# A hybrid encoder step on one core: normed tokens split in place, layer 1's weight sums started later, turned probabilities copied earlier

## The reference

```python
h = rmsnorm(x, g_pre_mix)
z = h @ w_in                       # B, C, xin | c_q, c_kv, k_rope | gate_conv, gate_mla
y_a = B * causal_conv3(C * xin)
y_b = latent_attention(...)        # 8 heads, chunk-causal mask, rotary key, cache for the sample
x = x + rmsnorm((sigmoid(ga) * y_a + sigmoid(gb) * y_b) @ w_o, g_post_mix)
x = x + rmsnorm(square(relu(rmsnorm(x, g_pre_ffn) @ w1)) @ w2, g_post_ffn)
```

## Time and profile before

| | |
|---|---|
| median of three runs (lowest, highest) | 1723.73 us (1723.25, 1723.80) |
| time of the profiled execution | 1726.3 us |
| its span, first to last instruction | 1724.5 us |
| PE busy | 1705.7 us (99%) |
| DVE busy | 1309.3 us (76%) |
| ACT busy | 855.1 us (50%) |
| POOL busy | 122.3 us (7%) |
| mean granted TensorE clock | 0.997 of full speed |

### The profile page before, as it was taken

One profiled execution on the slowest core, in us unless ns is written; L12 is line 12 of the kernel. 1 busy time (PEld: TensorE's weight loads), 2 busy tenths in 40 slices (PEclk: granted clock), 3 DMA queues, 4 the chain that ended last, 5 costly groups with the idle time before them and its releaser, 6 DMA issues.

```text
span 1724.5 us, 31894 instructions
## 1 busy us (share of the span) xinstructions
PE 1705.7 (99%) x12735; PEld 1690.9 (98%) x12735; DVE 1309.3 (76%) x2514; ACT 855.1 (50%) x1665; POOL 122.3 (7%) x163
## 2 busy tenths in 40 slices
PE   9999999999999999999999999999999999999997
PEld 9998999999999999999999999999999999999997
DVE  7788787767798786668687797777678887777665
ACT  7625454545465454436366364545435536444452
POOL 1412121212210000000001000000000000000000
PEclk9999999999999999999999999999999999999998
DMA  7899898898762232323124454343532213322231
GB/s 239 198 212 244 214 209 211 178 249 235 163 129 97 89 96 86 99 86 111 60 84 149 148 166 139 114 121 112 171 117 98 99 37 111 98 86 87 74 99 55
DMA packets 90996, 231.54 MB, mean 134 GB/s; under 512 B 9824, under 2 KB 25440, under 8 KB 90848
## 3 DMA queue, kind: packets, MB, share of 16 engines
q1 hardware_dynamic: 71968, 185.45, 33.5%
q0 software_dynamic: 17600, 41.95, 13.8%
q10 hardware_dynamic: 1280, 2.10, 0.3%
HBM read 214.39 MB, written 57.02 MB: 157 GB/s over the span
## 4 chain that ended last, share of the span: by engine, by line
PE 94%; DMA 2%; DVE 2%; ACT 1%; SPq 1%; issue 0%; DVEq 0%; ACTq 0%
PE ring L811 19%; PE ring L813 19%; PE ring L812 19%; PE att L811 11%; PE att L813 11%; PE att L812 11%; PE att L3527 1%; DMA cache_pe_raw<-cache_pe_in 1%; PE att L806 1%; PE att L805 1%; DMA small_raw<-small_in 1%; DMA xs_lo_raw<-h_kept 1%; PE att L818 0%; ACT rope_s L1291 0%; PE att L3343 0%
## 5 line engine op out<-in xcount | busy, mean ns | idle before, releaser
L811 PE MATMUL ring<-xs_hi,w_lo 128*128 128x288 f32 x1872 | 556.6, 297 | 4.3 <-DVE xs_lo L2744 2.2
L813 PE MATMUL ring<-xs_hi,w_hi 128*128 128x288 f32 x1872 | 551.4, 295 | 0.0
L812 PE MATMUL ring<-xs_lo,w_hi 128*128 128x288 f32 x1872 | 551.3, 294 | 0.0
L2071 DVE TENSOR_TENSOR w_lo<-w_raw,w_hi 128x1024 fp32r<-128x1024 f32 (+1 forms) x364 | 370.0, 1035 | 37.3 <-ACT w_hi L1220 27.2
L811 PEld LDWEIGHTS ring<-xs_hi,w_lo 128*128 128x128 f32 x1872 | 351.6, 188 | 7.3 <-DVE ga L2355 2.4
L812 PEld LDWEIGHTS ring<-xs_lo,w_hi 128*128 128x128 f32 x1872 | 351.7, 188 | 1.4
L813 PEld LDWEIGHTS ring<-xs_hi,w_hi 128*128 128x128 f32 x1872 | 351.5, 188 | 0.0
L813 PE MATMUL att<-f_hi,w_hi 128*128 128x288 f32 x960 | 283.2, 295 | 0.0
L812 PE MATMUL att<-f_lo,w_hi 128*128 128x288 f32 x960 | 282.9, 295 | 0.0
L811 PE MATMUL att<-f_hi,w_lo 128*128 128x288 f32 x960 | 282.6, 294 | 0.0
L811 PEld LDWEIGHTS att<-f_hi,w_lo 128*128 128x128 f32 x960 | 180.4, 188 | 0.0
(11 more groups left out here) (342 smaller groups left out, 3184.4 us busy)
## 6 DMA issues: line engine op xcount, KB each, us to landing
w_raw<-blocks_in SPq DMA_DIRECT2D x195, 512.0 KB, 3.7
weight_sums<-blocks_in POOLq DMA_DIRECT2D x80, 256.0 KB, 7.2
w_raw<-blocks_in SPq DMA_DIRECT2D x62, 256.0 KB, 4.6
weight_sums<-blocks_in POOLq DMA_DIRECT2D x20, 512.0 KB, 5.6
weight_sums<-weight_sums POOLq DMA_DIRECT2D x40, 256.0 KB, 7.6
w_raw<-weight_sums SPq DMA_DIRECT2D x20, 512.0 KB, 4.6
w_raw<-weight_sums SPq DMA_DIRECT2D x40, 256.0 KB, 4.4
small_raw<-small_in SPq DMA_DIRECT2D x16, 320.0 KB, 4.6
```

The lines of the kernel that those rows point to most:

```text
L811: pe.matmul(out, w[1], x[0], start=first, stop=False)
L812: pe.matmul(out, w[0], x[1], start=False, stop=False)
L813: return pe.matmul(out, w[0], x[0], start=False, stop=last)
L2071: return dve.tensor_tensor(out, a, hi.bitcast(F32), ALU.subtract)
```

## The change

The normed tokens are no longer stored and loaded back: ACT and DVE split them from `x` where they lie, in the order (0, 0), (4, 0), (0, 1), (4, 1) of half tiles. For this, in mixed head 2, the first two products come ahead of the projections on PE; the turned tiles are copied in head 2, each when the part of `x` under it has been split; their four low parts are made by DVE in head 2 as well, as is the weight of position 2, which was split at the end of head 1. Three low parts of the normed tokens are made at the end of head 1. In all plain heads ACT copies the turned probabilities ahead of the next weight and the small weights. POOL makes layer 1's ten sums only when head 7 of layer 0 has had its merged rows back. In head 7 the natural cache (`naraw`) is split behind the merged rows for w_o, the copy for the convolution comes ahead of the cache's sample columns, and the low parts of seven merged rows come ahead of the eighth.

```diff
@@ H_ORDER
-H_ORDER = ((0, 0), (4, 0), (4, 1), (0, 1))
+H_ORDER = ((0, 0), (4, 0), (0, 1), (4, 1))
@@ SP
-            def h_load(n):
...
-            def h_store(n):
...
-                if h == 1:
-                    sp.wait_ge(pl.h_made, KC * (L + 1))
...
-                    if (h, j) == (FIRST_MIXED - 1, 4):
-                        sp.wait_ge(pl.ring_full, full(L, r_hd(h, 4, 0)))
-                        sp.wait_ge(pl.h_stored, 48 * (L + 1))
-                        h_load(0)
-                        h_load(1)
-                        sp.wait_ge(pl.ring_full, full(L, r_hd(h, 4, 1)))
-                        h_load(2)
-                        h_load(3)
-                    elif is_mixed(h):
+                    if is_mixed(h):
@@ POOL
-        sums_steps(0, BEFORE_KEYS)
+        sums_steps(0, BEFORE_KEYS, 0, 2 * MIXED)
...
             if L == 0:
-                sums_steps(BEFORE_KEYS, N_SUMS + 2)
+                sums_steps(BEFORE_KEYS, 2 * MIXED + 2, 0, 2 * MIXED)
+                pool.wait_ge(pl.sums_third, 16 * 2 * MIXED)
+                pool.wait_ge(pl.my_landed, 64)
+                sums_copy(2 * MIXED)
+                sums_steps(2 * MIXED, N_SUMS + 2, 2 * MIXED, N_SUMS)
@@ ACT, plain_head
                 exponents(h)
+                turned_hi(h)
                 next_weight(2)
                 small_hi(L, h + 1)
-                turned_hi(h)
...
+                eng.wait_ge(pl.ring_free, ring_freed(3, 1))
+                apart()
+                conv_begin(h)
+                if h == HEADS - 1:
                     eng.wait_ge(pl.latent_lo, L * 4 + 4)
...
-                    eng.wait_ge(pl.nat_landed, L * 16 + 16)
-                    act.activation(pl.nah[:, :, :], pl.naraw[:, :, :], ACT.Copy).then_inc(pl.cache_hi, 1)
-                eng.wait_ge(pl.ring_free, ring_freed(3, 1))
-                apart()
-                conv_begin(h)
-                next_weight(3)
-                if h == FIRST_MIXED - 1:
-                    eng.wait_ge(pl.turn_made, 4 * (L + 1))
-                    eng.wait_ge(pl.h_stored, 48 * (L + 1))
-                    for t in TURN_ORDER:
-                        act.activation(pl.th[t][:, :, :], pl.traw[t][:, :, :], ACT.Copy).then_inc(pl.turn_hi, 1)
-                else:
+                if h != FIRST_MIXED - 1:
+                    next_weight(3)
                     next_weight(4)
@@ ACT, mixed_head
                 def normed_hi(n):
...
-                    eng.wait_ge(pl.h_landed[n], 16 * (L + 1))
-                    act.activation(pl.xh[tile], pl.xlraw[tile], ACT.Copy).then_inc(pl.h_hi, 1)
+                    eng.wait_ge(pl.ring_full, full(L, r_hd(h - 1, 4, half)))
+                    eng.wait_ge(pl.h_made, KC * (L + 1))
+                    act.activation(pl.xh[tile], pl.x[tile], ACT.Copy).then_inc(pl.h_hi, 1)
+
+                def turned_hi_of(i):
+                    t = TURN_ORDER[i]
+                    eng.wait_ge(pl.turn_made, 4 * (L + 1))
+                    eng.wait_ge(pl.h_lo, 4 * L + (3 if t < 2 else 4))
+                    act.activation(pl.th[t][:, :, :], pl.traw[t][:, :, :], ACT.Copy).then_inc(pl.turn_hi, 1)
 
                 def even_projections():
                     for half in range(2):
                         rotary_swap(h, half)
                     if h == FIRST_MIXED:
-                        normed_hi(0)
+                        turned_hi_of(1)
                     keys_hi(h)
                     rotary_hi(h)
...
                     if h == FIRST_MIXED:
-                        normed_hi(2)
+                        turned_hi_of(2)
+                        turned_hi_of(3)
+                        pos_hi(L, at + 2)
...
                 if h == FIRST_MIXED:
+                    for n in range(4):
+                        normed_hi(n)
+                    turned_hi_of(0)
+                    snapshot(0)
                     even_projections()
                     pos_hi(L, at + 3)
-                    normed_hi(3)
-                    snapshot(0)
@@ ACT, after weight_hi(L, n_wo(4), ...)
+            eng.wait_ge(pl.nat_landed, L * 16 + 16)
+            act.activation(pl.nah[:, :, :], pl.naraw[:, :, :], ACT.Copy).then_inc(pl.cache_hi, 1)
@@ DVE, plain_head
-                next_weight(3)
+                if h != FIRST_MIXED - 1:
+                    next_weight(3)
                 if h < FIRST_MIXED - 1:
                     next_weight(4)
-                elif h == FIRST_MIXED - 1:
-                    head_mix_lo(0)
-                    head_mix_lo(1)
 
                 attention_out(h)
 
                 own.wait()
+                if h == FIRST_MIXED - 1:
+                    normed_head_lo(0)
                 if h < HEADS - 1:
                     gated_out(h, 0)
+                    if h == FIRST_MIXED - 1:
+                        normed_head_lo(1)
                     gated_out(h, 1)
+                    if h == FIRST_MIXED - 1:
+                        normed_head_lo(2)
@@ DVE, mixed_head
                     rotary_sum(h, 0)
                     rotary_sum(h, 1)
+                    keys_lo(h)
                     if h == FIRST_MIXED:
-                        normed_head_lo(0)
-                    keys_lo(h)
+                        head_mix_lo(0)
                     rotary_lo(h)
-                    if h == FIRST_MIXED:
-                        normed_head_lo(1)
                     values_lo(h, 0)
                     values_lo(h, 1)
                     if h == FIRST_MIXED:
-                        head_mix_lo(2)
+                        head_mix_lo(1)
...
                 if h == FIRST_MIXED:
+                    upper_left(0, pl.cv[:, cols(0)])
+                    normed_head_lo(3)
                     even_projections()
+                    pos_lo(L, at + 2)
+                    head_mix_lo(2)
                     head_mix_lo(3)
-                    upper_left(0, pl.cv[:, cols(0)])
+                    first_difference(0)
                     pos_lo(L, at + 3)
-                    first_difference(0)
-                    normed_head_lo(2)
                     second_sum(0)
-                    normed_head_lo(3)
@@ DVE, w_o
+            for k in range(HEADS - 1):
+                merged_lo(x_part(L, X_WOA + k), k, cols(0))
             k = HEADS - 1
             gated_out(k, 0)
...
-            for k in range(HEADS - 1):
-                merged_lo(x_part(L, X_WOA + k), k, cols(0))
...
             weight_lo(L, n_wo(4), SLOT_WO[4])
+            cache_lo(2, pl.nal[:, :, :], pl.naraw[:, :, :], pl.nah[:, :, :])
@@ PE, mixed_head
-                if h == FIRST_MIXED:
-                    projections(h)
-                for i in range(4):
+                ahead = 2 if h == FIRST_MIXED else 4
+                for i in range(ahead):
                     product(h, 0, i)
-                if h != FIRST_MIXED:
-                    projections(h)
-                for i in range(4, 7):
+                projections(h)
+                for i in range(ahead, 7):
                     product(h, 0, i)
```

More of the change, by code:

```diff
@@ L954, in pos_load @@
                     sp.dma_start(pl.half_slot(s, k)[2], piece).then_inc(pl.slots[s], 16)
-            def h_load(n):
-                k0, half = H_ORDER[n]
-                sp.dma_start(pl.xlraw[:, k0:k0 + 4, cols(half)], pl.h_kept[:, k0:k0 + 4, cols(half)]) \
-                    .then_inc(pl.h_landed[n], 16)
-            def h_store(n):
-                rows = slice(3 * n, min(3 * n + 3, KC))
-                sp.dma_start(pl.h_kept[:, rows, :], pl.x[:, rows, :]).then_inc(pl.h_stored, 16)
             def my_load(n):
@@ L1014, in _ @@
                             pos_load(q)
-                    if h == FIRST_MIXED - 1 and j < 3:
-                        h_store(j)
                     if h == HEADS - 1:
@@ L1142, in sums_add_third, with sums_steps @@
             pool.dma_start(pl.sums[n][:, 3, :], pl.sums[n][:, 0, :], accum_op=ALU.add).then_inc(pl.sums_third, 16)
-        def sums_steps(n0, n1):
+        def sums_steps(n0, n1, first, end):
             for n in range(n0, n1):
-                if n < N_SUMS:
+                if n < end:
                     pool.wait_ge(pl.sums_copied, 48 * (n + 1))
-                if 1 <= n <= N_SUMS:
+                if first < n <= end:
                     pool.wait_ge(pl.sums_first, 32 * n)
-                if 2 <= n <= N_SUMS + 1:
+                if first + 1 < n <= end + 1:
                     pool.wait_ge(pl.sums_second, 16 * (n - 1))
-                if n >= 3:
+                if n > first + 2:
                     pool.wait_ge(pl.sums_third, 16 * (n - 2))
-                if n + 1 < N_SUMS:
+                if n + 1 < end:
                     sums_copy(n + 1)
-                if n < N_SUMS:
+                if n < end:
                     sums_add_first(n)
-                if 1 <= n <= N_SUMS:
+                if first < n <= end:
                     sums_add_second(n - 1)
-                if n >= 2:
+                if n > first + 1:
                     sums_add_third(n - 2)
```

(16 more changed lines are left out.)

4 lines of the change are left out of this document (removed).

## The result

| | before | after |
|---|---|---|
| median of six runs each (lowest, highest) | 1723.76 us (1723.25, 1729.72) | 1732.65 us (1730.76, 1735.46) |
| time of the profiled execution, its span | 1726.3, 1724.5 us | 1732.8, 1731.0 us |
| PE busy | 1705.7 us | 1709.6 us |
| mean granted TensorE clock | 0.997 | 0.995 |

The ratio after to before is 1.0039 (95% interval 1.0026 to 1.0052), 6.7 us by the ratio. The changed kernel is slower. The prediction was 1726.4 us with a range up to 1729.5, and the time lies above it.

What follows compares the result with a forecast made beforehand. PE, busy 1705.7 of 1724.5 us, was taken as the bound, with only 6.8 us of standstills to win. Terms -2.4 + 1.2 + 2.9 - 2.2 + 3.2 = +2.7 us on the median 1723.7 gave 1726.4 us, range 1719.5 to 1729.5.

Steps and rivals of the forecast that it cites:

- Turned probabilities, -2.4: Layer 0, head 1: copied ahead of the small weights, their low parts end before PE asks; 2.4 us of wait go.
- Head 2, layer 0, +1.2: Scores at T + 27.1 instead of T + 25.9, T being the end of head 1's last block's first half; 1.2 us lost.
- Head 2, layer 1, +2.9: PE waits 2.05 and 1.55 us for turned low parts; scores at T + 27.1 instead of T + 24.2, 2.9 us lost.
- the third rival: Head 2: PE does not wait for the turned tiles, all 6.8 us go; 1716.9 us, 1720.1 with harmful sums; 15%.
- The second matrix, +3.2: Layer 0, w2: moved sums delay the fifth weight load at 512, making w2(1, 0) late; bounds 0 and 4.4, taken 3.2 us.
- The equal turns: At w2's loads: queues share the DMA engines equally, landings double, 5.8 us late; 1729.0 us, 10%.
- w_o, -2.2: Layer 0, w_o: the cache's low part moves behind the merged rows, so PE's wait of 2.2 us for them goes.
- sums are harmless: Rival: layer 1's moved sums cost nothing in the feed-forward; 1723.2 us, 25%.
- The small weights still land late: Rival: head 2 of layer 0 starts 1.4 us later; 1727.8 us, 8%.

Runs made afterwards that it cites:

- filled: Changed kernel with sums as before, plus useless matmuls filling PE's waits in front of products 3 and 4 of head 2: 1727.03 us, 1.0006 (sums late: 1.0028).
- two parts alone: Kernel before with only turned probabilities first and the changes at head 7 and w_o; head 2 and sums as before: 1724.66 us, ratio 0.9986.
- the two reordered kernels: Changed kernel, sums as before, position 2's weight split at head 1's end, turned tiles' parts earlier in head 2: 0.9981; with further such moves: 0.9962.

## Why the prediction was wrong

The stretches of the first profile sum to 7.8 us where 2.7 were forecast. Of the 5.1 between, 2.4 lie in head 2 of layer 1, 1.4 in the stretch of w_o, 1.1 in that of the second matrix and 0.4 in head 2 of layer 0, less 0.2 at the probabilities.

**Turned probabilities, -2.4: right in place and size** (-2.6 in every profile). Left out was that the next head's transfers don't come earlier with PE; half of it goes in the old order too.

**Head 2, layer 0, +1.2: right** (+1.6). Scores at T + 27.3, forecast T + 27.1; waits of 2.35 and 1.3 us, forecast 2.05 and 1.55. But the old order, with PE as early, costs +1.4 and +1.3 there too, by late transfers. So little of this cost is the new order's own, and the term's being right owes something to luck.

**Head 2, layer 1, +2.9: this is the step that failed, and it measured +5.3.** Its bookkeeping was good: filled, scores come at T + 27.35, forecast T + 27.1, so the waits cost 3.3. Missing was what a wait does to PE after it. "3.6 of new waits less 0.4 of old ones" priced a standstill at its own length. The clock at 0.50 behind it added 2.0 us in this head, in this profile and two others; in a fourth the slow stretch was half as long and added nothing. That the third rival (PE does not wait) was held likelier than any dearer outcome of this head was wrong too.

**The second matrix, +3.2: right in cause, too small, and at another wait** (+4.3 and +6.0; removing the sums removes it all). I looked for the fifth load and a slack of 0.85 us at w2(1, 0). It was the first load, at which ACT stood 2.2 us (4.2 in the second profile), and everything behind it was late; PE stood for the norm factor, which had 0.37 us to spare, and w2(1, 0) was in time. That the term came near in size is luck in part. And it was not one place: the first pair's weights at 566 came late as well, by 1.3 to 2.0 us in three of four profiles. In the first profile part of it is the clock: w2's first 288 matmuls took 39.9 us at first, 38.4 in the second profile. "What was clean between 505 and 600 becomes shared" should have priced every load with little slack there. The equal turns of the Trainium skill (DMA: Bandwidth & Descriptors, Queues, rings and completion order), worked out to landings of 16.0 us and a wait of 5.8, overstate the landings (11.2 and 12.3) and lie near the whole cost of the stretch; the trace doesn't show them as such.

**w_o, -2.2: the wait went, the gain is not steady.** The ledger has -0.8 and -1.9 for the stretch with the heads before it. With the sums late four profiles gave -0.8, -0.8, -1.3 and -1.9; without them in the way -2.1, -2.1, -2.4, -2.5, but also 0.0, -0.4 and +1.8, where weights landed late for ACT and PE waited for merged rows or the sample's probabilities. What decides that stays open. The wait for the sample's probabilities was 1.5, 1.4, 0.9 and 0.5 us in the four profiles with the sums late; without them it was 1.6 (in two pieces) in one and 0.3 or less in six. So the sums may have a part in it, which no run shows.

In ratios, two parts alone 0.9986, with the sums late 1.0010, with the new head 2 as well 1.0038 (mean of two): the sums cost 4 us and head 2's order 5 us, each by some 3 us to either side, both off a gain of 2.4.

The rivals: "sums are harmless" is refuted by two kernels. "PE does not wait for the turned tiles" was false for this order, but true for another with the same work, one weight of it back at the end of head 1: splitting in place gains when DVE works in order of need (0.9962 against 0.9986 for the two parts alone), and DVE's order lost it here. "The small weights still land late" held in the old order of head 2 (2.4 us of ACT's waiting for them with two parts alone); in the changed kernel ACT copied them at 129.15 without a wait.

## What to carry to other kernels

When the bounding engine is TensorE, price a new standstill of about 2 us at more than its length (here up to 2.0 us more in one head), and look at the granted clock behind it, not only at the waits. Look at the clocks of all executions of the old kernel too: its one profile may show none of what it loses. When an engine is full in a stretch, list for each of its pieces who needs it next and when: the same DVE work in order of need, one weight of it split earlier, took PE's waits in layer 1 from 3.0 us to none. Background transfers moved to a "quiet" place cost there whatever slack the loads beside them lack, at every load of the stretch and not only at the nearest one.

## What the runs showed of the hardware that was not expected

The granted clock of TensorE fell to 0.50 for some 3 to 7 us, at standstills of 2.0 to 3.1 us, during them or up to 2 us behind them, in a program that keeps PE busy for 99% of its span, but not each time. In head 2 of layer 1 it fell at 2.35 us in four profiles and stayed at 1.00 behind 2.44 us in a fifth; at w2 it fell behind 1.99 us and not behind 3.02; in head 2 of layer 0 it fell in one of five, at waits of 2.34 to 2.43 us. In 33 executions of the two reordered kernels and of two parts alone, whose profiles have no wait over 1.8 us, one has a mean clock under 0.997. That the level is 0.50 and that activity keeps it away agrees with the Trainium skill (TensorE: Matmul & The Clock Gate, Part 1: The HAM clock gate). The filling shows the cause, but what chooses between two like waits stays open. A fall also isn't always a loss: where a second wait follows, the slow matmuls only fill it. In head 2 of layer 0 scores came at T + 27.33 with a fall and at T + 27.33 to 27.35 without (same order, sums early or late); in layer 1 at T + 27.36 with a fall of 3.4 us and T + 29.35 to 29.44 with one of 6.8.
